# Expert weights with every 128th row in a partition, and transposes of neighbouring columns

## What is computed

```
def expert_block(args):
    xi, e = args
    h = jax.nn.silu(xi @ w_gate[e]) * (xi @ w_up[e])
    return h @ w_down[e]
```

## Time and profile before

| what | value |
|---|---|
| median of three runs | 1070.37 us (1069.04 to 1071.2) |
| profiled execution, its own time | 1073.34 us |
| its span | 1071.6 us |
| mean granted TensorE clock | 0.936 |
| busy: TensorE matmul / weight load | 923.1 us / 630.1 us |
| busy: VectorE, ScalarE, GpSimd | 420.0, 272.1, 128.9 us |
| DMA | 266.85 MB in 87172 packets, mean 249 GB/s |

### The profile page before, as it was taken

The page is one execution under the profiler, slowest core; times in us unless marked ns, Lnnn a source line. Parts: engine busy times, 40 slices in busy tenths (PEclk is TensorE's granted clock), DMA queues, the critical chain, the costliest instruction groups (busy, mean ns, idle before and its releaser), DMA issues.

```text
span 1071.6 us, 14344 instructions
## 1 busy us (share of the span) xinstructions
PE 923.1 (86%) x5825; PEld 630.1 (59%) x5825; DVE 420.0 (39%) x874; ACT 272.1 (25%) x519; POOL 128.9 (12%) x206
## 2 busy tenths in 40 slices
PE   5999999899999999999359998887887888788743
PEld 4999999898899989999323333332322333233211
DVE  3764877775556544522712111111111111111176
ACT  3546454444353422212302111101101110110111
POOL 2000300000000010030221221111111101110003
PEclk8999999889999999999659999999999899999976
DMA  9214622212212423374877999999999999999952
GB/s 282 90 51 79 175 84 76 77 41 79 80 44 75 86 80 79 98 282 171 329 270 319 418 423 423 419 421 423 423 419 422 421 422 420 424 420 423 410 203 80
DMA packets 87172, 266.85 MB, mean 249 GB/s; under 512 B 29351, under 2 KB 60211, under 8 KB 66594
## 3 DMA queue, kind: packets, MB, share of 16 engines
q1 hardware_dynamic: 80066, 250.64, 60.4%
q0 software_dynamic: 7040, 15.28, 3.8%
HBM read 261.06 MB, written 15.16 MB: 258 GB/s over the span
## 4 chain that ended last, share of the span: by engine, by line
PE 51%; DMA 33%; DVE 7%; SPq 3%; ACT 3%; issue 1%; POOL 1%; POOLq 0%; DVEq 0%; ACTq 0%
PE ps L768 29%; DMA slot<-in_w_up 27%; PE ps L1062 9%; PE ps L1087 5%; SPq L492 2%; DMA raw<-in_w_o 2%; DMA x_half<-zn 2%; PE ps L810 1%; PE ps L892 1%; PE ps L858 1%; PE ps L882 1%; DMA st<-in_state_lru_h 1%; PE ps L1046 1%; DVE hL L1499 1%; POOL zT L644 1%
## 5 line engine op out<-in xcount | busy, mean ns | idle before, releaser
L1062 PE MATMUL ps<-slot,xt 128*64 128x512 f32 x512 | 251.7, 642 | 65.0 <-DMA slot<-in_w_up 62.6
L1063 PE MATMUL ps<-slot,xt 128*64 128x512 f32 x512 | 252.2, 643 | 0.0
L1062 PEld LDWEIGHTS ps<-slot,xt 128*64 128x64 f32 x512 | 70.2, 146 | 215.9 <-issue 169.9
L768 PE MATMUL ps<-xTh,wh 128*128 128x260 f32 x704 | 148.7, 293 | 0.0
L768 PE MATMUL ps<-xTl,wh 128*128 128x260 f32 x704 | 144.0, 287 | 0.0
L768 PE MATMUL ps<-xTh,rawL 128*128 128x260 f32 x704 | 144.0, 287 | 0.0
L1898 DVE TENSOR_TENSOR xt<-ps,g 128x512 f32<-128x512 f32 x32 | 22.1, 692 | 298.8 <-PE ps L1046 298.8
L1087 PE MATMUL ps<-slot,hT 128*64 128x512 f32 x512 | 116.9, 598 | 1.4 <-DVE hT L1909 1.4
L1418 DVE TENSOR_TENSOR rawL<-raw,wh 128x1024 fp32r<-128x1024 f32 x68 | 84.1, 1241 | 82.6 <-ACT wh L1150 82.2
L768 PEld LDWEIGHTS ps<-xTh,wh 128*128 128x128 f32 x704 | 111.7, 193 | 3.3 <-issue 2.2
L768 PEld LDWEIGHTS ps<-xTl,wh 128*128 128x128 f32 x704 | 111.3, 193 | 0.0
(11 more groups left out here) (320 smaller groups left out, 1238.5 us busy)
## 6 DMA issues: line engine op xcount, KB each, us to landing
slot<-in_w_gate SPq DMA_DIRECT2D x64, 1024.0 KB, 29.2
slot<-in_w_up SPq DMA_DIRECT2D x64, 1024.0 KB, 32.1
slot<-in_w_down SPq DMA_DIRECT2D x32, 2048.0 KB, 33.2
raw<-in_w_in SPq DMA_DIRECT2D x18, 1024.0 KB, 5.1
raw<-in_w_in SPq DMA_DIRECT2D x16, 256.0 KB, 4.5
raw<-in_w_lru_out SPq DMA_DIRECT2D x4, 1024.0 KB, 5.0
raw<-in_w_attn_out SPq DMA_DIRECT2D x16, 256.0 KB, 4.5
raw<-in_w_o SPq DMA_DIRECT2D x4, 1024.0 KB, 5.4
```

Of the source, the lines that this page charges most:

```text
L768: last = mm(out_of[:, a, 0:HT], w[:, k, :], x[:, k, a * HT:(a + 1) * HT], start=(k == 0 and n == 0), stop=(k == KT - 1 and n == 2))
L1062: mm(out[0:CAP, :], tokens, w[:, q, :], start=start, stop=stop)
L1063: last = mm(out[CAP:P, :], tokens, w[:, 4 + q, :], start=start, stop=stop)
```

## The change

The rows of a partition are no longer neighbours: a partition p of a gate or up half gets the rows p, p + 128, p + 256 and p + 384, and the same for `w_down`. The bytes and the number of DMAs stay the same; a DMA now has four runs for each partition, of 2 KB (gate and up) and 4 KB (down). TensorE's q-th step therefore multiplies with the rows 128q to 128q + 127, and the transposes take 128 neighbouring columns. With that order the scale and offset stand in `col` as they are needed: `g8` and `b8` become views of `col`, their two loads go, and VectorE's wait falls from 96 to 64.

```
-        g8 = at("g8", [P, 2, 4], F32, oK + 2752)
-        b8 = at("b8", [P, 2, 4], F32, oK + 2784)
+        g8 = col[:, R_G1:R_B1].rearrange("p (h q) -> p h q", h=2)
+        b8 = col[:, R_B1:NVEC].rearrange("p (h q) -> p h q", h=2)
...
-                        src = A[w][bass.ds(e, 1), c * (D // 2):(c + 1) * (D // 2), :].rearrange("e (p j) f -> p (e j f)", p=P)
-                        sp.dma_start(dst[:, 4 * n:4 * n + 4, :].rearrange("p j f -> p (j f)"), src).then_inc(signal, 16)
+                        src = A[w][bass.ds(e, 1), c * (D // 2):(c + 1) * (D // 2), :].rearrange("e (j p) f -> p (e j) f", p=P)
+                        sp.dma_start(dst[:, 4 * n:4 * n + 4, :], src).then_inc(signal, 16)
                 else:
-                    src = A["w_down"][bass.ds(e, 1), :, :].rearrange("e (p j) d -> p (e j d)", p=P)
-                    sp.dma_start(dst[:, :, :].rearrange("p a b -> p (a b)"), src).then_inc(signal, 16)
+                    src = A["w_down"][bass.ds(e, 1), :, :].rearrange("e (j p) d -> p (e j) d", p=P)
+                    sp.dma_start(dst[:, :, :].rearrange("p (j a) b -> p j (a b)", a=2), src).then_inc(signal, 16)
...
-                    sp.dma_start(g8[:, :, :], A["ln1_g"].rearrange("(h p q) -> p h q", h=2, q=4)).then_inc(s_ln, 16)
-                    sp.dma_start(b8[:, :, :], A["ln1_b"].rearrange("(h p q) -> p h q", h=2, q=4)).then_inc(s_ln, 16)
...
-                    last = nc.tensor.transpose(bank[0][:, q * P:(q + 1) * P], src[:, q:512:4], ident[:, :])
+                    last = nc.tensor.transpose(bank[0][:, q * P:(q + 1) * P], src[:, q * P:(q + 1) * P], ident[:, :])
...
-                    last = nc.tensor.transpose(bank[4][:, q * P:(q + 1) * P], src[:, q:512:4], ident[:, :])
+                    last = nc.tensor.transpose(bank[4][:, q * P:(q + 1) * P], src[:, q * P:(q + 1) * P], ident[:, :])
...
-                    dve.wait_ge(s_ln, 96)
+                    dve.wait_ge(s_ln, 64)
```

## The result

The changed kernel takes **1098.6 us** (median of four runs, 1098.21 to 1099.53) against 1069.7 us (four runs, 1068.74 to 1071.2): a ratio of **1.027, interval 1.0252 to 1.0288**. The forecast was 1078.5 us with a range to 1092: the direction was right, the size was not. The profiled execution took 1098.39 us, its span is 1096.6 us.

The account below looks back on a forecast made before the run. The prediction took the weight loads' bytes and rate to bound the kernel from 576.20 us on. Terms 14.8 + 0.5 - 4.2 - 2.0 - 1.0 = +8.1 us gave a median of 1078.5 us, range 1065 to 1092.

Parts of the forecast that it names:

- What bounds it: Experts from chunk 12 on, after 576.20 us: loads run without a gap, so bytes left and their rate set the end.
- Runs: Weight loads of 28 experts after 576 us: 120 more packets per engine and expert at 4.4 ns each, +14.8 us.
- the gather: First token gather before the experts: waits behind chunk 5's packets, which become 4 KB instead of 16 KB; -2.0 us.
- the head: Chunks 0 to 2, loaded ahead of the last half-chunk of w_o, take longer; +0.5 us.
- the transposes: Three groups of L1046 before 576.20 us and one of L1074 in the tail: neighbouring columns save 0.26 us a group; -1.0 us.
- the store: Store of x1 ahead of the experts: its packets take turns with weight packets, which become smaller; -4.2 us.
- Packets are free: Rival, stretch after 576 us: in a full queue packets cost nothing extra, only the gains stay; -7.2 us, 1063.2; chance 0.15.
- Far runs are dear: Rival, weight loads: distance between runs costs, so 2 KB runs reach only 384 GB/s; +23.9 us, 1094.3; chance 0.08.
- The turns do not get shorter: Rival, store and gather: engines finish one transfer's runs before switching queues, so both wait as now; +14.3 us, 1084.7; chance 0.17.
- The rest: g8 and b8 loads leaving SP's queue, VectorE's shorter wait, copy_xt's multiplies and SP's longer issues: no effect.

Follow-up runs that it names:

- m2: Kernel of weight loads only, layer left out: 1 MB loads without a pause, one at a time, or four under way; 349 GB/s at 1 KB runs, 387 at 2 KB.
- m1: Kernel of weight loads only, layer left out: stages with long, short, near and far runs; 387 GB/s at 2 KB, 411 at 4 KB, near or far.
- e3: Kernel before, with gate and up in 2 KB runs of every second row, 4 KB apart; down and transposes as before; 1096.73 us, ratio 1.0245.
- e2: Kernel before, with only w_down in 4 KB runs and its hidden-value transposes on neighbouring columns; gate and up as before; 1074.89 us, ratio 1.0045.
- b2: Kernel before, without an edit, run for a second profile; 1070.01 us, span 1068.2 us.
- v2: Kernel before, with chunk 9 issued when the stores of x1 have landed, chunks 8 and 5 when the first gather has landed; 1064.36 us, ratio 0.9941.
- m3: Kernel of loads only, layer left out: 2 KB runs from SP's queue alone, then half from SP's and half from ScalarE's; no faster with two queues.

## Why the prediction was wrong

**What bounds it: right.** The stretch behind chunk 12 follows the weights' rate; it alone became 30.1 us longer, where the whole span became 28.4 us longer.

**Runs, the step that failed.** "+14.8 us" came from "4.4 ns a packet", a line through two bursts; it measured +30.1 us, 9.0 ns. Of the 20.3 us between the forecast's +8.1 and the +28.4 of the two profiles, 15.3 are this term's; the gather has 2.1, the head 2.0, the transposes 1.0 and the store 0.7, the first row of the table takes 1.4 back, and 0.6 are spread over the other rows. The mechanism was right and the price wrong, because the bursts were no sample of the stretch. The first microseconds run faster (m2), and the 1 KB bursts by more, 385 GB/s against 349 in a steady stream, than the 4 KB one, 416 against 411. That tilts the line. The check with the steady rate, 15.05 to 14.9 us, stood at the end with 40 packets an expert, where 4.4 or 9.4 ns each differ by 0.2 us. It also took the queue's share for time, and records of packets overlap: the share is 1.05 in m2's 2 KB stream and 1.10 in its 1 KB stream, where nothing else runs.

The Trainium skill (DMA: Bandwidth & Descriptors, Why small descriptors are slow) puts a packet's fixed overhead at about 3 bus cycles, an estimated 3.5 ns at its 850 MHz for the fabric; the steady streams measured 9.4, and the measurement decides. The Trainium skill (DMA: Bandwidth & Descriptors, Where 436 GB/s comes from) gives 435.2 GB/s as what the 16 ports into SBUF can carry; 36.6 ns per 1000 B on each of 16 engines is 437, which agrees.

**Packets are free: fell.** In m1 each shorter run has the lower rate, 430, 424, 411 and 387 GB/s.

**Far runs are dear: its time was the nearest, 1094.3, by luck, and its reason fell.** The steady 2 KB rate, 387, happens to be about the 384 that this rival took from the 1 KB bursts, but m1 and e3 have the same rate for near runs. So the sign that the prediction gave for it, a rate under 400, did not tell it from a dearer packet. The other sign, a smaller share of w_up loads in the chain, does not tell what bounds the stretch: the share fell from 27% to 24% with DMA still full, and in e2 the chain goes through SP's issues instead (L492, 29%).

**The turns do not get shorter: fell for the store, held for the gather.** Both queues of after from 532 to 534, as the earlier trace rows:

```profile
q1 hardware_dynamic: 108, 0.44, 53.7%
q0 software_dynamic: 109, 0.41, 49.5%
```

One for one again, with smaller packets on q1. The store measured -3.5 us against b2 and -5.2 against the first profile; the forecast said -4.2. The gather did not gain its -2.0. Its first packet came 4.4 us after its issue in both kernels. The weight queue's packets in that time, in before (543.35 to 547.9), after (539.06 to 543.5) and v2 (537.38 to 539.6):

```profile
q1 hardware_dynamic: 96, 1.57, 84.8%
```

```profile
q1 hardware_dynamic: 764, 1.76, 103.3%
```

```profile
q1 hardware_dynamic: 57, 0.34, 36.1%
```

Eight times as many packets go ahead of it in after, but nearly the same bytes. What a gather waits for beside a full queue before its first packet is thus not a number of turns; with only 0.34 MB of weights in front it began after 2.2 us (v2). I had taken the store's rule for it.

**The head: +0.5, measured +2.5.** From chunk 0's issue to w_o's landing it is 22.97 us, 21.64 in b2, so +1.3, which the steady price explains: 120 packets an engine at 9.4 ns are 1.1 us. The other 1.2 us is TensorE's clock. In after TensorE did nothing from 485 to 487, where b2 has 0.21 us of work, and had worked for 1.78 us of the three before, where b2 has all three; then the granted clock fell to 0.50, the lower level of 1.2 GHz, about a microsecond sooner (0.69 from 487 to 489, where b2 has 1.00), and the ten L951 matmuls took 2.25 us for b2's 1.30. This part is not the change's alone: v2, with long runs, has 2.35 us for the same ten.

**Transposes: -1.0, at most -0.4.** Weight loads of L1044 and L1072 in after (the earlier trace rows before):

```profile
L1044 PEld LDWEIGHTS ps<-ident,xg x128: 138/140/229, 546.1 to 1029.0; 128*128 128x128 f32 x128
...
L1072 PEld LDWEIGHTS ps<-ident,gu x128: 137/141/143, 558.5 to 1046.6; 128*128 128x128 f32 x128
```

They fell as forecast, but four transposes overlap: a group took 0.70 us, less than its four weight loads of 209 ns together. So a group fell from 0.70 to about 0.6 us, not by 0.26, and an expert from 11.95 to 11.77 with two groups in it. From the gather's landing to chunk 12 nothing shows (25.04 and 25.08).

**The rest: a statement was wrong, at little cost.** "Nothing is behind it but the next weights": the loads of x1 for the last residual (L538, in after L536) stand there too. SP issued them from 988.54 on in before and from 985.20 on in b2; in after the weights held SP until 1030.36. VectorE's first work on them, in after, in b2 and in the first profile of before (idle time in front, and what ended it):

```profile
1049.67 1.21 DVE L1923 TENSOR_TENSOR xr<-xr,lnG 8x1024 f32<-8x1024 f32 x1 [1.37 <-DMA xr<-x_half]
```

```profile
1021.47 1.21 DVE L1925 TENSOR_TENSOR xr<-xr,lnG 8x1024 f32<-8x1024 f32 x1 [1.25 <-DMA xr<-x_half]
```

```profile
1024.56 1.21 DVE L1925 TENSOR_TENSOR xr<-xr,lnG 8x1024 f32<-8x1024 f32 x1 [0.96 <-DMA xr<-x_half]
```

VectorE is busy from there almost to the end, so these loads are on the path in after, but they are in b2 as well (2% of its chain). The change adds 0.1 us of idle time against b2 and 0.4 against the first profile.

What stays open is why loading starts faster than it goes on: m2 excludes the depth of the queue, between four loads and sixteen, and m3 the making of descriptors for one queue as the limit of the steady rate. What in the shared path makes 9 ns a packet stays open as well. No run tells more.

## What to carry to other kernels

Take the price of a packet from a stream as long as the stretch it is for, never from bursts of a megabyte, and test it at the end where there are many packets. In these loads from HBM into SBUF a run's length sets the rate, on either side, and its place does not, in steps of 4 to 512 KB. A change of layout that shortened runs in a stretch bound by DMA cost 9 ns for each added packet on each engine. Small packets in a bulk queue do help another queue's store, but holding the bulk loads back until the small transfers have landed (v2) helped more, 5.6 us in all, and cost the stream 1.2 us.

## What the runs showed that was not expected

- Pieces of 2 KB in SBUF cost as much as runs of 2 KB in HBM (387 GB/s, m1).
- Steps of 256 KB (2 KB runs) and 512 KB (4 KB runs) in a partition cost nothing against near ones. The Trainium skill (DMA: Bandwidth & Descriptors, Latency and other measured facts) has copies between HBM tensors at 164 GB/s at a row pitch of 2 MiB and at 103 at 4 MiB, where it calls 214 full. Its pitch is the one between partitions; the loads of m1 have 2 to 32 KB there, so no run here shows that.
- The first microseconds of loading run faster, if unevenly: 2 KB loads with four under way at 405 GB/s over three microseconds, then at 387 (m2); 1 KB loads at 385 in the first, 349 in the long run.
- A gather beside a full weight queue has its first packet 4.4 us after its issue, after 1.6 to 1.8 MB of the other queue's data, whatever the size of the packets.
- With runs of 2 KB a weight load lands 15.5 us after its issue (median of w_gate's, 29.2 before): the full queue holds fewer bytes (an estimate from the weight queue's rates: 15.5 us at 376 GB/s are 5.8 MB, 29.2 at 403 are 11.8), and SP stays 2.8 us on an issue for w_gate, 0.6 before (medians).
